# A mixture-of-experts router's product, turned round and laid between the transposes of a layer norm

## The chip, the cores and the metric

One NeuronCore of a Trainium2 chip runs the whole program in one launch. The metric is the device time of one execution in microseconds (us). The core's engines run side by side, each in the order of its own instructions, and wait for one another by semaphores: TensorE (PE; its weight loads are listed apart as PEld), VectorE (DVE), ScalarE (ACT), GpSimdE (POOL), and SyncE (SP), which issues most of the loads.

## The reference, cut to what matters

512 tokens with 1024 features pass through two layers of one kind of block and then two of another. The change is in the second kind, between its first layer norm and its experts:

```python
def route(x2, w_router, router_bias):                 # x2: 512 x 1024
    scores = jax.nn.sigmoid(jnp.einsum('nd,de->ne', x2, w_router))   # 512 x 16
    biased = scores + router_bias
    ...                                                # best group, two experts, weights
for l in range(DEPTH):                                 # DEPTH = 2
    mix = token_mixing(...)
    x = layer_norm_2(DN_ALPHA_2 * x + mix, ln1_g[l], ln1_b[l])
    ffn = moe(x.reshape(B * S, D), w_router, router_bias, w1[l], w3[l], w2[l])
    x = layer_norm_2(DN_ALPHA_2 * x + ffn, ln2_g[l], ln2_b[l])
```

Everything is float32. Which experts a token goes to is decided from these scores, so no expert's work can start before them.

## The kernel before, in words

The 512 tokens are four tiles of 128 (`NT`), the 1024 features eight blocks of 128 (`KC`). A full-precision product is made of three: each operand is split into a high part in the type fp32r and a low part (the rest), and high times high, high times low and low times high are added up in a bank of PSUM.

The layer norm is written out over three engines. VectorE (`norm_v`) handles tile after tile: it adds the rows of the residual (line 614), takes the moments (618, 622), and applies mean, gain, deviation and bias (644, 651); line 651 raises `norm_z`. TensorE (`norm_pe`, line 681) then turns the tile's eight 128x128 blocks into banks 2i and 2i+1 and raises `norm_tr` once for each bank. ScalarE (`norm_a`, line 666) copies a bank into `xT_hi`, the high part with features on the partitions and tokens on the free axis, and VectorE (line 627) makes `xT_lo` and raises `norm_lo`. ScalarE takes its deviations two tiles ahead (line 661), in order, so it makes the high part of tile i only when tile i+2 has its variance. On VectorE the low part of tile i-1 stands behind line 651 of tile i and the variance of tile i+1.

After the norm comes the router, on TensorE at lines 2024 to 2034: wait for all eight low parts; 24 products (lines 468 to 470, `triple`) with the router's weights (128x16) stationary and 512 tokens moving, into 16 rows of bank 0; wait for the sigmoid that ScalarE writes into `scT` (line 2272, 16x512); turn `scT` back in four transposes of 16x128 (line 2033) into bank 2. VectorE copies that to `rsc` (line 2494, 128x64) and starts a chain of small operations: the bias (2497), the best group, two best experts as one-hot rows (up to 2540). TensorE ranks the tokens with two products (2037, 2038), VectorE works out the slots, TensorE places them (2042), and GpSimdE gathers the rows of the experts' tokens. The experts' first products (2070) follow.

Ahead of the router, ScalarE issues four loads on its own queue: the next norm's gain and bias, then `rbias` (2269) and `row128` (2270). VectorE waits for the last two before line 2497. The router's weights are loaded and split by GpSimdE in the ring of weight units; that is done before the norm ends.

Of the kernel before, what the change touches and what calls it, by code (L numbers as in the profile page):

```python
# [20 lines left out]
P = 128  # L21
S = 512
NT = S // P
D = 1024
KC = D // P
# [6 lines left out]
ACT = mybir.ActivationFunctionType  # L32
# [18 lines left out]
NE, NG = 16, 4  # L51
NOV = 2 * S // P
NB = NOV + NE
RAW, SPLIT = 4, 2
# [9 lines left out]
def shape_constants():  # L64
# [75 lines left out]
    "m_t": (0, 0, 16),  # L140
    "m_o": (0, 0, 16),
    "a_ot": (0, 0, 4),
    "rt_tr": (0, 0, 1),
    "rt_rank": (0, 0, 1),
    "slot_mm": (0, 0, 1),
    "gb_ld": (2, 4, 4),
# [37 lines left out]
    "h_hi": (0, 0, 17),  # L184
    "y_ev": (0, 0, 33),
    "gt_use": (0, 0, 26),
    "v_step": (24, 237, 343),
    "norm_var": (4, 8, 8),
    "norm_z": (4, 8, 8),
    "norm_lo": (8, 16, 16),  # L190
# [211 lines left out]
class Feed:  # L402
# [3 lines left out]
    RAW, SPLIT = 12, 4  # L406
# [59 lines left out]
def triple(pe, out, wh, wl, xh, xl, first, last):  # L466

    pe.matmul(out, wh, xh, start=first, stop=False)
    pe.matmul(out, wh, xl, start=False, stop=False)
    return pe.matmul(out, wl, xh, start=False, stop=last)  # L470


def flat(ap):
    return ap.rearrange("p a b -> p (a b)")
# [6 lines left out]
def build(nc, t, out):  # L481

    ctx = ExitStack()
    with ctx:
# [6 lines left out]
        def signal(name, step=1):  # L491
            return Signal(name, sem(name), step)
# [3 lines left out]
        h = sb("h", [P, NT, D])  # L496
        xT_hi = sb("xT_hi", [P, KC, S], F32R)
        xT_lo = sb("xT_lo", [P, KC, S], F32R)
        ring = Stream(sb, sem)
# [15 lines left out]
        eps, unit1 = small[:, 0:1], small[:, 1:2]  # L515
        ident = konst[:, K_ID:K_ID + P]
        bank = [ctx.enter_context(nc.psum_tensor(f"bank{i}", [P, S], F32)) for i in range(8)]
# [49 lines left out]
        v_step, a_step = signal("v_step"), signal("a_step")  # L567
# [3 lines left out]
        norm_var, norm_sd, norm_z = signal("norm_var"), signal("norm_sd"), signal("norm_z")  # L571
        tile_sum = signal("tile_sum")
        norm_tr, norm_hi, norm_lo = signal("norm_tr"), signal("norm_hi"), signal("norm_lo")
# [84 lines left out]
        def norm_a(A, n):  # L658
# [12 lines left out]
            for i in range(NT):  # L671
                if i + 2 < NT:
                    deviation(i + 2)
                high(i)

        def norm_pe(T, n):
            for i in range(NT):
                T.eng.wait_ge(norm_z.sem, norm_z.at(T, NT * n + i + 1))
                for x in range(2):
                    for k in range(4):  # L680
                        last = T.eng.transpose(bank[2 * i + x][:, k * P:k * P + P],  # L681
                                               h[:, i, (4 * x + k) * P:(4 * x + k + 1) * P], ident)
                    last.then_inc(norm_tr.sem, norm_tr.up(T))

        def load_gb(A, g_row, b_row):
            A.eng.dma_start(gb[:, 0, :], over(g_row, [P, D])).then_inc(gb_ld.sem, gb_ld.up(A))
# [616 lines left out]
        def vector1(V):  # L1303
# [240 lines left out]
        U2_IW, U2_V, U2_MK, U2_PW, U2_MV, U2_G, U2_OUT, U2_R = 5, 14, 26, 30, 31, 35, 83, 91  # L1544
# [37 lines left out]
        s7 = lambda name, shape, dt=F32: sb(name, shape, dt, moe)  # L1582
# [11 lines left out]
                      for w, x in ((wt_hi, xT_hi), (wt_lo, xT_lo))))  # L1594
        yg = [wt[:, i, :] for i in range(2 * NT)]
        rsc, rbi = s7("rsc", [P, NT, NE]), s7("rbi", [P, NT, NE])
        scT, row128 = s7("scT", [NE, S]), s7("row128", [P, P])
        rgs, ghot, rbest = s7("rgs", [P, NT, NG]), s7("ghot", [P, NT, NG]), s7("rbest", [P, NT, 1])
        slot_ge, slot_b, slot_p = (s7(n, [P, 2 * NT, w]) for n, w in (("slot_ge", NB + 2), ("slot_b", NB + 1), ("slot_p", P)))
        hot2, d128 = s7("hot2", [P, NT, NE]), s7("d128", [P, 2 * NT])  # L1600
# [3 lines left out]
        gw = s7("gw", [P, NT, 4])  # L1604
# [31 lines left out]

        m_s, m_mx, m_p, m_t, m_te, m_o = (signal(n) for n in ("m_s", "m_mx", "m_p", "m_t", "m_te", "m_o"))

        gt_sig, gt_use, mg_hi, mg_lo, rt_sc, rt_oh, rt_rank, rt_dest, be_ok, rt_tr, slot_oh, slot_mm = (signal(n) for n in (
            "gt_sig", "gt_use", "mg_hi", "mg_lo", "rt_sc", "rt_oh", "rt_rank", "rt_dest", "be_ok", "rt_tr", "slot_oh", "slot_mm"))  # L1640

        x_tr, x_hi, x_lo, act_h, h_val, h_tr, h_hi, h_lo, y_ev, yg_use = (signal(n) for n in (
            "x_tr", "x_hi", "x_lo", "act_h", "h_val", "h_tr", "h_hi", "h_lo", "y_ev", "yg_use"))
# [164 lines left out]
        def tensor2(T):  # L1808
            pe = T.eng
# [38 lines left out]
            for c in range(ROPED):  # L1848
# [5 lines left out]
                if c == 4:  # L1854
                    wh, wl = (w[:, 0:64].rearrange("p (k c) -> p k c", k=KC) for w in ring.weights(T, U2_IW))
# [16 lines left out]
            for j in range(4):  # L1872
                wh, wl = ring.weights(T, U2_V + j)
# [147 lines left out]
            for _ in dense:  # L2021
                pass
            rows_products(T, U2_OUT, KC, xT_hi, xT_lo, mg_lo)
            norm_pe(T, 0)
            T.eng.wait_ge(norm_lo.sem, norm_lo.at(T, 8))

            wh, wl = (w[:, 0:P].rearrange("p (k e) -> p k e", k=KC) for w in ring.weights(T, U2_R))
            for k in range(KC):
                last = triple(pe, bank[0][0:NE, :], wh[:, k, :], wl[:, k, :], xT_hi[:, k, :], xT_lo[:, k, :], k == 0, k == 7)
            last.then_inc(ring.done, 1)  # L2030
            T.eng.wait_ge(rt_sc.sem, T.alone(rt_sc.at(T, 1)))
            for i in range(NT):
                last = pe.transpose(bank[2][:, NE * i:NE * i + NE], scT[:, i * P:i * P + P], ident[0:NE, 0:NE])
            last.then_inc(rt_tr.sem, rt_tr.up(T))
            T.eng.wait_ge(rt_oh.sem, rt_oh.at(T, 1))

            pe.matmul(bank[1][:, 0:NT * NE], konst[:, K_TRF:K_TRF + P], flat(oh[:, 2, :, :]), start=True, stop=True)
# [113 lines left out]
        def scalar2(A):  # L2151
# [116 lines left out]
            load_gb(A, t["ln2_g_2"][bass.ds(l, 1), :], t["ln2_b_2"][bass.ds(l, 1), :])  # L2268
            act.dma_start(rbias[:], over(t["router_bias_2"].rearrange("(o n) -> o n", o=1), [P, NE])).then_inc(rb_ld.sem, rb_ld.up(A))
            act.dma_start(row128[:], t["konst"][:, K_END:K_END + P]).then_inc(rb_ld.sem, rb_ld.up(A))  # L2270
            A.eng.wait_ge(ring.done, ring.products(A, U2_R))
            act.activation(scT[:], bank[0][0:NE, :], ACT.Sigmoid).then_inc(rt_sc.sem, rt_sc.up(A))

            def x_high(e):
                for y in range(2):
# [48 lines left out]
        def vector2(V):  # L2324
            v = V.eng
# [164 lines left out]
                v.tensor_tensor(xT_lo[:, k, :], merged[k], xT_hi[:, k, :].bitcast(F32), SUB).then_inc(mg_lo.sem, mg_lo.up(V))  # L2490
            norm_v(V, 0, U2_OUT + KC - 1)

            V.eng.wait_ge(rt_tr.sem, rt_tr.at(V, 1))
            v.tensor_copy(flat(rsc[:]), bank[2][:, 0:NT * NE]).then_inc(v_step.sem, v_step.up(V))
            V.eng.wait_ge(v_step.sem, v_step.last(V))
            V.eng.wait_ge(rb_ld.sem, rb_ld.at(V, 2))
            v.tensor_tensor(rbi[:], rsc[:], over(rbias[:].unsqueeze(1), [P, NT, NE]), ADD).then_inc(v_step.sem, v_step.up(V))
            V.eng.wait_ge(v_step.sem, v_step.last(V))
# [327 lines left out]
```

## Time and profile before

| | |
|---|---|
| time, median of 3 runs | 3400.06 us (3392.2 to 3403.74) |
| the profiled execution | 3393.37 us, its span 3391.6 us |
| mean granted clock of TensorE | 0.928 of full |
| PE / PEld busy | 2981.4 us (88%) / 2356.0 us (69%) |
| DVE / ACT / POOL busy | 1815.1 / 1381.4 / 1145.3 us |
| the chain that ended last, by engine | PE 57%, issue 20%, DVE 9%, POOL 8%, ACT 3% |

The span runs from the first to the last instruction of the profiled execution. The granted clock is the share of TensorE's full clock (2.4 GHz) that the chip lets through; it is 1.00 or 0.50 at any moment, so the engine works at 2.4 or at 1.2 GHz. Busy times count an engine's instructions, for PE with ends that overlap. The chain is followed back from the last instruction, at each step to what released it. Times of a row are counted from the start of the span.

### The profile page before, as it was taken

Reading aid. Unit: us, or ns where it says so; the run is one execution under the profiler, and the core shown is the slowest. Engines: PE = TensorE matmul, PEld = TensorE weight load, DVE = VectorE, ACT = ScalarE, POOL = GpSimd, SP = SyncE. Lnnn points to the kernel's source line nnn. Section 1 sums busy time; section 2 is a strip of 40 time slices with the busy share of each in tenths; the row PEclk is TensorE's granted clock in tenths of the full one; section 3 lists DMA queues with packets and bytes.
Section 4 is the critical chain, followed back from the end, with each engine's and each line's share of the span. In section 5 each row is a group of like instructions: output and inputs, shape, how many; then the busy total and the mean of one; then the engine's idle time right before and its main releaser. Section 6 shows DMA issues by size and latency. Waiting matters only on the chain.

```text
span 3391.6 us, 44938 instructions
## 1 busy us (share of the span) xinstructions
PE 2981.4 (88%) x13284; PEld 2356.0 (69%) x13284; DVE 1815.1 (54%) x2681; ACT 1381.4 (41%) x1973; POOL 1145.3 (34%) x699
## 2 busy tenths in 40 slices
PE   6887899979987999889999976999499999959994
PEld 4666688866756888766777764887357777738883
DVE  3774434035754432246544246998556533159996
ACT  3523455215342553111244214887121343118883
POOL 2213344533123445433743530110345543611101
PEclk8998899989988999988999987999699999969996
DMA  3211233522112334322322335998222322339993
GB/s 111 64 34 62 81 99 93 173 68 70 38 53 76 94 99 137 119 69 57 103 66 57 85 142 199 411 411 334 91 67 72 94 57 68 99 141 383 411 411 146
DMA packets 373732, 461.46 MB, mean 136 GB/s; under 512 B 33396, under 2 KB 280262, under 8 KB 373512
## 3 DMA queue, kind: packets, MB, share of 16 engines
q1 hardware_dynamic: 353664, 392.05, 34.3%
q0 software_dynamic: 14976, 54.53, 4.2%
q10 hardware_dynamic: 4872, 12.26, 1.0%
q8 instruction: 100, 1.64, 0.2%
q14 instruction: 120, 0.98, 0.1%
HBM read 423.10 MB, written 35.65 MB: 135 GB/s over the span
## 4 chain that ended last, share of the span: by engine, by line
PE 57%; issue 20%; DVE 9%; POOL 8%; ACT 3%; DMA 1%; POOLq 0%; DVEq 0%; ACTq 0%; SPq 0%
PE bank L462 8%; PE bank L463 7%; POOL unit_lo L382 6%; PE bank L1935 4%; PE bank L2070 3%; PE bank L2071 3%; PE bank L2074 3%; PE bank L701 2%; PE bank L2084 2%; PE bank L2088 2%; PE bank L2085 2%; DVE u L1343 2%; PE bank L797 2%; PE bank L798 1%; PE bank L800 1%
## 5 line engine op out<-in xcount | busy, mean ns | idle before, releaser
L462 PE MATMUL bank<-xT_hi,unit_hi 128*128 128x512 f32 x1680 | 692.1, 412 | 20.7 <-DVE xT_lo L627 10.5
L463 PE MATMUL bank<-xT_lo,unit_hi 128*128 128x512 f32 x1680 | 664.9, 396 | 0.0
L382 POOL TENSOR_TENSOR unit_lo<-unit_raw,unit_hi 128x1024 fp32r<-128x1024 f32 (+1 forms) x168 | 402.6, 2396 | 762.9 <-ACT unit_hi L375 762.9
L365 POOL TENSOR_SCALAR unit_hi<-unit_raw 128x1024 fp32r<-128x1024 f32 (+1 forms) x208 | 201.7, 970 | 759.5 <-PE bank L1935 303.3
L367 POOL TENSOR_TENSOR unit_lo<-unit_raw,unit_hi 128x1024 fp32r<-128x1024 f32 (+1 forms) x208 | 442.2, 2126 | 17.4
L462 PEld LDWEIGHTS bank<-xT_hi,unit_hi 128*128 128x128 f32 x1680 | 322.2, 192 | 119.7 <-issue 42.7
L463 PEld LDWEIGHTS bank<-xT_lo,unit_hi 128*128 128x128 f32 x1680 | 322.3, 192 | 70.6 <-issue 7.3
L375 ACT ACTIVATE unit_hi<-unit_raw 128x1024 fp32r<-128x1024 f32 (+1 forms) x168 | 176.7, 1052 | 415.9 <-PE bank L701 174.6
L701 PE MATMUL bank<-xT_hi,unit_lo 128*128 128x512 f32 x1040 | 256.9, 389 | 0.0
L447 DVE TENSOR_TENSOR wt_lo<-wt,wt_hi 128x1024 fp32r<-128x1024 f32 x192 | 229.2, 1222 | 33.0 <-ACT wt_hi L442 32.1
L681 PE MATMUL bank<-konst,h 128*128 128x128 f32 x288 | 69.0, 419 | 201.6 <-DVE h L651 201.6
L447 DVE TENSOR_TENSOR xT_lo<-wt,xT_hi 128x1024 fp32r<-128x1024 f32 x192 | 234.5, 1223 | 12.5 <-ACT xT_hi L442 2.7
L442 ACT ACTIVATE xT_hi<-wt 128x1024 fp32r<-128x1024 f32 x192 | 203.6, 1063 | 50.8 <-PE bank L2074 32.5
L701 PEld LDWEIGHTS bank<-xT_hi,unit_lo 128*128 128x128 f32 x1040 | 195.2, 188 | 40.5
L614 DVE SCALAR_TENSOR_TENSOR h<-h,bank 128x512 f32<-128x512 f32 x48 | 30.6, 678 | 353.1 <-PE bank L800 353.1
L442 ACT ACTIVATE wt_hi<-wt 128x1024 fp32r<-128x1024 f32 x192 | 200.4, 1063 | 33.0 <-PE bank L2074 27.5
L681 PEld LDWEIGHTS bank<-konst,h 128*128 128x128 f32 x288 | 55.0, 218 | 216.2 <-DVE h L651 209.2
L1524 DVE SCALAR_TENSOR_TENSOR cv<-bank,pcol,cv 128x511 f32<-128x511 f32 x88 | 66.0, 750 | 242.5 <-ACT cv L1258 242.5
L1753 POOL DMA_INDIRECT xb<-h_rows,slots x32 | 44.0, 1376 | 383.3 <-PE bank L2049 243.1
L661 ACT ACTIVATE sd<-mv,small 128x1 f32<-128x1 f32 x36 | 10.6, 295 | 364.8 <-DVE mv L622 364.8
L797 PE MATMUL bank<-unit_hi,g_hi 128*128 128x512 f32 x352 | 137.4, 390 | 3.6 <-POOL unit_lo L382 3.6
L798 PE MATMUL bank<-unit_hi,g_lo 128*128 128x512 f32 x352 | 137.0, 389 | 0.0
(453 smaller groups left out, 6204.6 us busy)
## 6 DMA issues: line engine op xcount, KB each, us to landing
wt<-in_w SPq DMA_DIRECT2D x384, 512.0 KB, 8.1
unit_raw<-in_w_in SPq DMA_DIRECT2D x276, 256.0 KB, 3.1
unit_raw<-in_w_ffn_up SPq DMA_DIRECT2D x176, 256.0 KB, 3.1
unit_raw<-in_w_ffn_down SPq DMA_DIRECT2D x88, 256.0 KB, 3.1
unit_raw<-in_w_out SPq DMA_DIRECT2D x64, 256.0 KB, 2.8
y_rows<-yb POOLq DMA_DIRECT2D x32, 512.0 KB, 7.3
y_rows<-zeros POOLq DMA_DIRECT2D x24, 512.0 KB, 5.2
unit_raw<-in_w_br SPq DMA_DIRECT2D x96, 128.0 KB, 2.2
```

What stands on the lines that cost most here:

```text
L365: pool.eng.tensor_scalar(hi, raw, 1.0, 0.0, MUL, ADD).then_inc(self.hi_made, 1)
L367: pool.eng.tensor_tensor(lo, raw, hi.bitcast(F32), SUB).then_inc(self.split, 1)
L375: act.eng.activation(self.hi[j % SPLIT][:, 0:width], self.raw[j % RAW][:, 0:width], ACT.Copy).then_inc(self.hi_made, 1)
L382: pool.eng.tensor_tensor(lo, raw, hi.bitcast(F32), SUB).then_inc(self.split, 1)
L442: act.eng.activation(self.hi[n % self.SPLIT], self.raw[n % self.RAW], ACT.Copy).then_inc(self.hi_made, 1)
L447: dve.eng.tensor_tensor(self.lo[n % self.SPLIT], self.raw[n % self.RAW], self.hi[n % self.SPLIT].bitcast(F32), SUB).then_inc(self.split, 1)
L462: pe.matmul(out, wh, xh, start=first, stop=False)
L463: pe.matmul(out, wh, xl, start=False, stop=False)
L701: last = T.eng.matmul(out_bank[:, 0:n], wl[:, k, :], xh[k], start=False, stop=k == kc - 1)
L797: T.eng.matmul(o, x_hi[:, row, c], wh[:, n], start=k == 0, stop=False)
L798: T.eng.matmul(o, x_lo[:, row, c], wh[:, n], start=False, stop=False)
L1935: last = pe.matmul(o, wl[:, k, :], ah[k], start=False, stop=k == kc - 1)
```

## The change: what it does

The roles of the operands are exchanged. A tile of 128 tokens (of `xT_hi` or `xT_lo`) is stationary and the router's 16 columns move, so that the scores come out with tokens on the partitions, 16 columns of bank 0 for each tile. The product of tile i-1 stands in TensorE's order between the transposes of tile i and those of tile i+1; the last two products follow the last transposes. ScalarE takes one sigmoid of 128x64 straight into `rsc`, and VectorE waits for that. `scT`, the four transposes back, their semaphore and VectorE's copy are gone. ScalarE takes a sigmoid of one column into an unused column of `gw` ahead of its wait for the product.

```diff
+        def turned_rows(T, n, i):
+            T.eng.wait_ge(norm_z.sem, norm_z.at(T, NT * n + i + 1))
+            for x in range(2):
+                for k in range(4):
+                    last = T.eng.transpose(bank[2 * i + x][:, k * P:k * P + P],
+                                           h[:, i, (4 * x + k) * P:(4 * x + k + 1) * P], ident)
+                last.then_inc(norm_tr.sem, norm_tr.up(T))
+
         def norm_pe(T, n):
             for i in range(NT):
-                ...
+                turned_rows(T, n, i)
...
-            norm_pe(T, 0)
-            T.eng.wait_ge(norm_lo.sem, norm_lo.at(T, 8))
-
-            wh, wl = (w[:, 0:P].rearrange("p (k e) -> p k e", k=KC) for w in ring.weights(T, U2_R))
-            for k in range(KC):
-                last = triple(pe, bank[0][0:NE, :], wh[:, k, :], wl[:, k, :], xT_hi[:, k, :], xT_lo[:, k, :], k == 0, k == 7)
-            last.then_inc(ring.done, 1)
-            T.eng.wait_ge(rt_sc.sem, T.alone(rt_sc.at(T, 1)))
+            def routed(i):
+                c = slice(i * P, i * P + P)
+                T.eng.wait_ge(norm_lo.sem, norm_lo.at(T, 2 * i + 2))
+                if i == 0:
+                    T.eng.wait_ge(ring.split, ring.split_is(T, U2_R))
+                wh, wl = (w[U2_R % SPLIT][:, 0:P].rearrange("p (k e) -> p k e", k=KC) for w in (ring.hi, ring.lo))
+                o = bank[0][:, i * NE:i * NE + NE]
+                for k in range(KC):
+                    pe.matmul(o, xT_hi[:, k, c], wh[:, k, :], start=k == 0, stop=False)
+                    pe.matmul(o, xT_hi[:, k, c], wl[:, k, :], start=False, stop=False)
+                    last = pe.matmul(o, xT_lo[:, k, c], wh[:, k, :], start=False, stop=k == KC - 1)
+                if i == NT - 1:
+                    last.then_inc(ring.done, 1)
+
             for i in range(NT):
-                last = pe.transpose(bank[2][:, NE * i:NE * i + NE], scT[:, i * P:i * P + P], ident[0:NE, 0:NE])
-            last.then_inc(rt_tr.sem, rt_tr.up(T))
+                turned_rows(T, 0, i)
+                if i:
+                    routed(i - 1)
+            routed(NT - 1)
...
+            act.activation(gw[:, 0, 3:4], unit1, ACT.Sigmoid)
             A.eng.wait_ge(ring.done, ring.products(A, U2_R))
-            act.activation(scT[:], bank[0][0:NE, :], ACT.Sigmoid).then_inc(rt_sc.sem, rt_sc.up(A))
+            act.activation(flat(rsc[:]), bank[0][:, 0:NT * NE], ACT.Sigmoid).then_inc(rt_sc.sem, rt_sc.up(A))
...
-            V.eng.wait_ge(rt_tr.sem, rt_tr.at(V, 1))
-            v.tensor_copy(flat(rsc[:]), bank[2][:, 0:NT * NE]).then_inc(v_step.sem, v_step.up(V))
-            V.eng.wait_ge(v_step.sem, v_step.last(V))
+            V.eng.wait_ge(rt_sc.sem, rt_sc.at(V, 1))
```

## Rows read from the trace of the kernel before

**Rows 1.** The page: shares of the chain that ended last, by engine.
```profile
PE 57%; issue 20%; DVE 9%; POOL 8%; ACT 3%; DMA 1%; POOLq 0%; DVEq 0%; ACTq 0%; SPq 0%
```
**Rows 2.** The chain, first layer's router: start us, us, engine, tile, line.
```profile
2031.89 1.30 DVE h L651
2033.23 1.98 PE bank L681 x8
...
2035.87 0.70 DVE xT_lo L627
2036.69 0.60 PE bank L468
...
2043.48 0.25 PE bank L470
2043.75 0.60 ACT scT L2272
2044.48 0.40 PE bank L2033 x4
2044.90 0.24 DVE rsc L2494
2045.16 0.24 DVE rbi L2497
```
**Rows 3.** The chain, second layer's router.
```profile
3004.79 1.30 DVE h L651
...
3018.01 0.23 DVE rbi L2497
```
**Rows 4.** The timeline of the first layer's norm: start, us, engine, line, operation.
```profile
2021.32 1.97 PE L681 MATMUL bank<-konst,h 128*128 128x128 f32 x8 [4.36 <-DVE h L651]
2022.23 1.29 DVE L627 TENSOR_TENSOR xT_lo<-bank,xT_hi 128x512 fp32r<-128x512 f32 x2 [0.84 <-ACT xT_hi L666]
...
2028.41 1.97 PE L681 MATMUL bank<-konst,h 128*128 128x128 f32 x8 [5.12 <-DVE h L651]
2029.32 1.29 DVE L627 TENSOR_TENSOR xT_lo<-bank,xT_hi 128x512 fp32r<-128x512 f32 x2 [0.85 <-ACT xT_hi L666]
2033.10 1.28 DVE L627 TENSOR_TENSOR xT_lo<-bank,xT_hi 128x512 fp32r<-128x512 f32 x2
```
**Rows 5.** The timeline of TensorE where the slots are placed.
```profile
2060.68 3.61 PE L2042 MATMUL bank<-slot_b,slot_p 128*128 128x25 f32 x16 [7.64 <-DVE slot_p L2593]
```
**Rows 6.** The timeline of TensorE in an earlier stage with 256 columns moving.
```profile
1650.61 1.12 PE L701 MATMUL bank<-b_hi,unit_lo 128*128 128x256 f32 x8
```
**Rows 7.** Groups by form: busy us, mean ns of one, idle before.
```profile
L2042 PE MATMUL bank<-slot_b,slot_p 128*128 128x25 f32 x32 | 7.2, 390 | 15.3 <-DVE slot_p L2593 15.3
...
L701 PE MATMUL bank<-b_hi,unit_lo 128*128 128x256 f32 x64 | 9.4, 289 | 0.7 <-POOL unit_lo L367 0.5
...
L469 PEld LDWEIGHTS bank<-c_lo,unit_hi 128*128 128x128 f32 x8 | 1.5, 189 | 0.7 <-issue 0.5
...
L469 PEld LDWEIGHTS bank<-xT_lo,unit_hi 128*8 128x8 f32 x16 | 1.4, 88 | 2.2
```
**Rows 8.** Windows: stretch, its us, busy (count) of PE, PEld, DVE, ACT, POOL; PEclk, DMA share, GB/s.
```profile
2022.40:2029.40 7.00, 1.88 (x10) 1.48 (x9) 6.15 (x11) 1.18 (x4) 0.00 (x0) 0.50 0.17 70
2036.60:2039.40 2.80, 2.71 (x7) 0.99 (x8) 0.00 (x0) 1.28 (x1) 0.00 (x0) 0.50 0.95 334
2039.60:2043.70 4.10, 4.10 (x18) 1.52 (x16) 0.00 (x0) 0.00 (x0) 0.00 (x0) 1.00 0.10 26
2060.60:2064.30 3.70, 3.61 (x16) 3.49 (x16) 0.02 (x1) 0.00 (x0) 0.00 (x0) 0.50 0.00 0
```
**Rows 9.** ScalarE and its queue ahead of the sigmoid, by the timeline.
```profile
2036.64 0.45 ACTq L2270 DMA_DIRECT2D row<-in_konst  x1
...
2037.19 1.28 ACT L2272 ACT_TABLE_LOAD   x1 [1.35 <-issue]
```
**Rows 10.** The tile `row128`: issue to landing in both layers.
```profile
DMA to landing us min/median/max: 4.1/4.9/5.8
```

More of the change, by code:

```diff
@@ L142 @@
     "a_ot": (0, 0, 4),
-    "rt_tr": (0, 0, 1),
     "rt_rank": (0, 0, 1),
@@ L186 @@
     "gt_use": (0, 0, 26),
-    "v_step": (24, 237, 343),
+    "v_step": (24, 237, 342),
     "norm_var": (4, 8, 8),
@@ L674, in norm_a @@
                 high(i)
+        def turned_rows(T, n, i):
[5 more added lines that the diff above has]
+                last.then_inc(norm_tr.sem, norm_tr.up(T))
         def norm_pe(T, n):
             for i in range(NT):
[L678 to L683, printed above, removed]
+                turned_rows(T, n, i)
         def load_gb(A, g_row, b_row):
@@ L1596, in build @@
         rsc, rbi = s7("rsc", [P, NT, NE]), s7("rbi", [P, NT, NE])
-        scT, row128 = s7("scT", [NE, S]), s7("row128", [P, P])
+        row128 = s7("row128", [P, P])
         rgs, ghot, rbest = s7("rgs", [P, NT, NG]), s7("ghot", [P, NT, NG]), s7("rbest", [P, NT, 1])
@@ L1637, in build @@
         m_s, m_mx, m_p, m_t, m_te, m_o = (signal(n) for n in ("m_s", "m_mx", "m_p", "m_t", "m_te", "m_o"))
-        gt_sig, gt_use, mg_hi, mg_lo, rt_sc, rt_oh, rt_rank, rt_dest, be_ok, rt_tr, slot_oh, slot_mm = (signal(n) for n in (
-            "gt_sig", "gt_use", "mg_hi", "mg_lo", "rt_sc", "rt_oh", "rt_rank", "rt_dest", "be_ok", "rt_tr", "slot_oh", "slot_mm"))
+        gt_sig, gt_use, mg_hi, mg_lo, rt_sc, rt_oh, rt_rank, rt_dest, be_ok, slot_oh, slot_mm = (signal(n) for n in (
+            "gt_sig", "gt_use", "mg_hi", "mg_lo", "rt_sc", "rt_oh", "rt_rank", "rt_dest", "be_ok", "slot_oh", "slot_mm"))
         x_tr, x_hi, x_lo, act_h, h_val, h_tr, h_hi, h_lo, y_ev, yg_use = (signal(n) for n in (
```

## The prediction
> **What bounds the kernel now.** I read the page first, then the chain of waits around the router, then the timeline of the norm ahead of it, then windows for TensorE's clock. The page's chain gives PE 57% of the span, VectorE 9% and ScalarE 3% [rows 1], so a change in one stage has to be read in that stage. At the router the chain passes through every instruction that the change touches: line 651 of the last tile, eight transposes, the last high and low part, 24 products from 2036.69 to 2043.73, the sigmoid, four transposes back, VectorE's copy, and the bias at 2045.16 [rows 2]. Nothing runs beside it that the end waits for, and the ranks, the slots, the gather and the experts follow from it. So what is gained or lost at line 2497 shows whole in the span, once in each of the two layers. The distance from line 651 of the last tile to line 2497 is 13.27 us in the first layer [rows 2] and 13.22 us in the second [rows 3]: one calculation serves both.
>
> The norm ahead of it is VectorE's. The transposes of tiles 1, 2 and 3 start at 2021.32, 2028.41 and 2033.23, each for some 2 us, and TensorE stands idle in between [rows 2, 4]. The low parts of tiles 0, 1, 2 and 3 are done at 23.52, 30.61, 34.38 and 36.57 (times of two digits are 2000 us and more) [rows 2, 4]. TensorE's clock is at 0.50, that is 1.2 GHz, all through these gaps [rows 8].
>
> **What goes.** From the end of the last product to line 2497 there are now 45.16 - 43.73 = 1.43 us: the sigmoid of 16x512 0.60, the transposes 0.40, the copy 0.24, and hand-overs [rows 2]. After the change one sigmoid of 128x64 stands there. Its 64 elements a partition are an eighth of 512. The trace has no such form; it costs between 0.1 and 0.6, and I take 0.3, as VectorE's 64-element operations cost 0.24 [rows 2]; with hand-overs 0.4. So 1.0 us goes (bounds 0.75 to 1.25). The table load of 1.28 us at 2037.19 was already hidden ahead of the wait [rows 9], and the one-column sigmoid follows it there: nothing gained, nothing lost, unless the product ended before 38.8.
>
> **What the product costs.** 24 instructions become 96, in four groups of 24, each with a weight load of 128 columns and 16 columns moving. Before, 512 moving columns covered a load of 16; now there is next to nothing to cover a load of 128. What does such a pair cost? The trace has no fp32r product with so few columns. Nearest is line 2042, 128 columns loaded and 25 moving, in f32: 16 of them in 3.61 us, the last with its own 0.39, so (3.61 - 0.39) / 15 = 0.215 us from start to start, at the low clock [rows 5, 7, 8]. Is fp32r as slow? At the full clock its load takes 189 ns for 128 columns and 88 ns for 8 [rows 7]: 0.84 ns a column, two cycles of 2.4 GHz. For 128 columns that is 108 ns at the full clock and 215 ns at the low one, the same as line 2042. From below the bound is four transposes with a load of 128 columns of 16 rows in 0.40 us, about half of it the last one's own time, so some 0.06 each at the full clock, 0.12 at the low one [rows 2, 8]. From above it is eight products with 256 moving columns in 1.12 us at the full clock, the last with its own 0.29, so 0.12 each, or 0.24 at the low one [rows 6, 7]. I take 0.215, being closest to line 2042, so 5.2 us for a tile at the low clock, 20.6 for the four, where 7.04 stood before.
>
> The Trainium skill, TensorE: Matmul & The Clock Gate, section "LDWEIGHTS (loading the stationary operand)", gives a load as its columns divided by 1.2 nanoseconds, so 107 ns for 128, and does not double it for this type or at the low clock. By it the four groups would take 10 us. Line 2042 at the low clock is twice that, so I put the row first, and the page's number is a rival below.
>
> **Which clock?** The product before raised it: from 2036.60 to 2039.40 PE is busy 2.71 of 2.80 us at 0.50, and after that the rows show 1.00 [rows 8]. But line 2042 keeps PE busy for 3.61 of 3.70 us with few columns moving, and the clock stays at 0.50 [rows 8]. The new product looks like line 2042, not like the old one. I take 0.50 throughout.
>
> **Where it lies.** TensorE works in order, so each group also stands in front of the next transposes.
> - Tile 0's product may start when its low part is made: 23.52 plus the 0.12 seen between the low part and the first product, 23.65. It ends at 28.8. Tile 2's transposes are due at 28.41, so they start 0.4 late, and TensorE is free at about 30.55. Their high parts are used by VectorE only at 33.10: hidden.
> - Tile 1's product waits for 30.61, starts at 30.7 and ends at 35.9. Tile 3's transposes were ready at 33.23. They now wait behind it: 2.7 us late. This is the new stall. Behind them on ScalarE stand the last high parts and the four loads of its queue, on VectorE the last low part: 36.57 becomes 39.3.
> - Tile 3's transposes hold TensorE for 1.7 us, to 37.6. Tile 2's product follows to 42.8, tile 3's to 48.0; nothing more is waited for, since the low part of 39.3 is long there. The last result comes 0.39 after its start, at 48.1.
> - Sigmoid and hand-overs 0.4: line 2497 at 48.5 against 45.16, which is 3.3 us later.
>
> In words: from 30.7 on TensorE has three groups of 5.2 us and one set of transposes in a row, 17.3 us, where it had the transposes and 7.04 us of products, most of them at the full clock. Nearly all of the overlap with the norm is eaten by 13.6 us more work (20.6 - 7.04). The loads of ScalarE's queue are issued 2.7 us later; `row128` took 5.8 us at most from its issue at 36.64 [rows 9, 10], so it is there at 45.1, ahead of 48.5. Its own moved DMAs, and the row stores that SP issues on `norm_z`, are hidden. The ring's semaphore for the router's unit is raised later, and no one else is due on it. The clock is at 0.50 for the ranks and slots in both cases [rows 8], so nothing follows there.
>
> **The sum.** 2 x 3.3 = 6.6 us on the profiled 3393.4: 3400.0. That execution is 6.7 under the median of 3400.06, so for a median I say 3406.7, in round figures 3406.
>
> **The rivals.**
> - *The clock rises.* If the dense new product lifts the clock as the old one did, a group costs 24 x 0.11 = 2.6 us from the second or third on. Tile 1's product ends at 33.4, the transposes of tile 3 start 0.2 late and go twice as fast, tile 2's product runs from 34.4 to 37.0, tile 3's to 39.6, line 2497 could go at 40.1. But then VectorE waits for `row128`: issued at 36.6, landed at 42.4 in the first layer and at the equal of 40.8 in the second [rows 9, 10]. Gain 2.7 + 4.3 = 7.0 us; time 3393. For it: the old product did so at the same share of busy time. Against it: line 2042. This is the case on the other side, and it turns on whether the granted clock reaches 1.00 before tile 2's product. The same page of the Trainium skill, section "What's actually happening", says that the throttled clock is the default and that activity releases it, which speaks for this rival if a busy PE with few columns counts as activity.
> - *Loads are cheaper than I think.* At 0.12 a pair, at the low clock, a group is 2.9 us: tile 0's ends at 26.6, tile 1's at 33.6, the last two run from 35.4 to 41.2, line 2497 is at 41.7, held in the first layer by `row128` to 42.4. Gain 2.7 + 3.5 = 6.2; time 3394. For it only the four small transposes, which load 16 rows. It decides below some 0.17 us a pair: 30.7 + 24 x 0.17 = 34.8, 1.5 late, the end at 44.7, as before.
> - *Something else than the product decides*, such as a landing or a phase of the experts' loads, and takes or gives a few us. Nothing in the chain points to one.
>
> **How the numbers follow.** Forecast 0.68, clock rises 0.15, cheaper loads 0.12, something else 0.05. A measurement of this kernel can tell some 0.3%, that is 10.2 us, from no change; all three cases lie within it. A quarter of the forecast's sizes (pairs up to 0.24: 24 x 0.025 x 3 = 1.8 us a layer more) and the spread of the runs (11.5 us from lowest to highest before) carry 0.14 of it beyond 10.2 us slower, and about a quarter of the two rivals beyond 10.2 faster. So faster 0.08, same 0.77, slower 0.15. The range takes in both rivals' 3393, less 4 for spread, and the top of the forecast, 3406 + 4 + 4: 3389 to 3414. The forecast's own range is 3401 to 3413.
>
> **What would show it.** In the changed profile: 96 products a layer, 0.215 us from start to start; windows over them at 0.50; tile 3's transposes some 2.7 us after line 651 instead of 0.06; from line 651 of the last tile to line 2497 16.6 us instead of 13.3; no wait of VectorE for `row128`. A granted clock of 1.00 over the last two groups, or pairs at 0.12, would make it wrong, and then line 2497 should stand 8 to 11 us behind line 651.

## The result, and the profile after

Over 20 runs each the changed kernel takes 3403.47 us in the median (3399.06 to 3408.27), the kernel before 3399.14 us (3392.20 to 3404.79). The ratio is 1.0015 with a 95% interval from 1.0008 to 1.0022: 5.1 us slower, between 2.7 and 7.5. That is real, and within the 0.3% that the forecast called no change. The profiled execution took 3403.39 us, its span is 3401.6 us.

The page's chain by engine has hardly moved (before: [rows 1]):

```profile
PE 58%; issue 20%; DVE 9%; POOL 8%; ACT 3%; DMA 1%; POOLq 0%; ACTq 0%; DVEq 0%; SPq 0%
```

The timeline of the first layer's norm and router in the changed kernel (start us, us, engine, line, operation, idle before and what ended it). Line numbers have shifted: 681 is now 679, 651 is 650, 627 is 626, 2497 is 2507; the product is lines 2035 to 2037.

```profile
2023.45 0.38 PE L2035 MATMUL bank<-unit_hi,xT_hi 128*128 128x16 f32 x1 [0.36 <-DVE xT_lo L626]
...
2028.38 0.36 PE L2037 MATMUL bank<-unit_hi,xT_lo 128*128 128x16 f32 x1
...
2028.59 1.97 PE L679 MATMUL bank<-konst,h 128*128 128x128 f32 x8
...
2030.47 0.38 PE L2035 MATMUL bank<-unit_hi,xT_hi 128*128 128x16 f32 x1
...
2031.70 1.28 DVE L650 SCALAR_TENSOR_TENSOR h<-h,rs,gb 128x1024 f32<-128x1024 f32 x1
...
2035.40 0.36 PE L2037 MATMUL bank<-unit_hi,xT_lo 128*128 128x16 f32 x1
...
2035.61 1.97 PE L679 MATMUL bank<-konst,h 128*128 128x128 f32 x8
...
2037.23 0.36 PE L2035 MATMUL bank<-unit_hi,xT_hi 128*128 128x16 f32 x1
...
2038.24 0.69 DVE L626 TENSOR_TENSOR xT_lo<-bank,xT_hi 128x512 fp32r<-128x512 f32 x1 [0.16 <-ACT xT_hi L665]
...
2039.50 1.28 ACT L2282 ACT_TABLE_LOAD   x1 [1.29 <-issue]
...
2040.80 0.20 ACT L2282 ACTIVATE gw<-small 128x1 f32<-128x1 f32 x1
...
2047.26 0.36 PE L2037 MATMUL bank<-unit_hi,xT_lo 128*128 128x16 f32 x1
2047.65 0.23 ACT L2284 ACTIVATE rsc<-bank 128x64 f32<-128x64 f32 x1 [6.66 <-PE bank L2037]
...
2047.91 0.22 DVE L2507 TENSOR_TENSOR rbi<-rsc,rbias 128x64 f32<-128x64 f32 x1 [8.98 <-ACT rsc L2284]
```

Read it beside [rows 2, 4]. Tile 0's product begins at 2023.45, as soon as its low part is made, and its last instruction starts at 2028.38. Tile 2's transposes follow at 2028.59. Tile 1's product begins at 2030.47, and its last instruction starts at 2035.40, while line 650 of tile 3 began at 2031.70 and was done at 2032.98: the transposes of tile 3 start only at 2035.61, without a gap behind the product, where they stood 0.06 us behind line 651 before. Then come two more groups of 24 in a row, and the last result meets a sigmoid of 0.23 us and, 0.26 after its start, the bias add at 2047.91. From line 650 (651 before) of the last tile to that add it is 16.21 us instead of 13.27 [rows 2]. The second layer repeats it: 3027.94 - 3011.74 = 16.20, instead of 13.22 [rows 3].

```profile
3011.74 1.28 DVE L650 SCALAR_TENSOR_TENSOR h<-h,rs,gb 128x1024 f32<-128x1024 f32 x1
...
3027.94 0.22 DVE L2507 TENSOR_TENSOR rbi<-rsc,rbias 128x64 f32<-128x64 f32 x1 [8.98 <-ACT rsc L2284]
```

Windows over tile 0's, tile 1's and the last two products (columns as in [rows 8]): PE and PEld are both busy without a hole, and the granted clock is 0.50 in all three.

```profile
2023.40:2028.60 5.20, 5.14 (x25) 5.15 (x25) 4.88 (x7) 0.29 (x2) 0.00 (x0) 0.50 0.00 0
2030.40:2035.60 5.20, 5.20 (x25) 5.13 (x24) 3.75 (x6) 0.60 (x1) 0.00 (x0) 0.50 0.27 107
2037.20:2047.40 10.20, 10.20 (x50) 10.20 (x48) 1.38 (x2) 2.24 (x4) 0.00 (x0) 0.50 0.34 110
```

Groups by form in the changed kernel. The weight load takes 333 ns, nearly the 361 ns of the product itself. Both are longer than the 0.213 us from one start to the next, since neighbouring instructions overlap in the trace.

```profile
L2036 PE MATMUL bank<-unit_lo,xT_hi 128*128 128x16 f32 x64 | 23.1, 361 | 0.0
...
L2036 PEld LDWEIGHTS bank<-unit_lo,xT_hi 128*128 128x128 f32 x64 | 21.3, 333 | 0.0
```

### The profile page after: what moved, and what is told of

Its sections match the earlier page's. It is cut to its first block, busy times and chain, and to the rows that moved or that the text cites. A ratio compares the mean times of both kernels' runs of the same rounds, so it can differ in the third digit from the quotient of the medians.

```text
span 3401.6 us, 45212 instructions
## 1 busy us (share of the span) xinstructions
PE 3008.8 (88%) x13420; PEld 2392.2 (70%) x13420; DVE 1814.6 (53%) x2679; ACT 1381.3 (41%) x1975; POOL 1144.1 (34%) x699
## 4 chain that ended last, share of the span: by engine, by line
PE 58%; issue 20%; DVE 9%; POOL 8%; ACT 3%; DMA 1%; POOLq 0%; ACTq 0%; DVEq 0%; SPq 0%
PE bank L461 8%; PE bank L462 7%; POOL unit_lo L381 6%; PE bank L1937 4%; PE bank L2081 3%; PE bank L2082 3%; PE bank L2085 3%; PE bank L703 2%; PE bank L2095 2%; PE bank L2099 2%; PE bank L2096 2%; DVE u L1345 2%; PE bank L799 2%; PE bank L800 1%; PE bank L802 1%
## 5 line engine op out<-in xcount | busy, mean ns | idle before, releaser
L660 ACT ACTIVATE sd<-mv,small 128x1 f32<-128x1 f32 x36 | 10.6, 295 | 363.9 <-DVE mv L621 363.9
```

## The experiments

The kernel before ran beside each of them on the same chip, with medians of 3398.6 to 3400.9, and the ratios are to those runs. "Distance" is always from the start of line 651 (or its like) of the last tile to the start of the bias add in the first / second layer, in us.

| kernel | median | ratio to before (95%) | distance |
|---|---|---|---|
| before | 3399.14 | 1 | 13.27 / 13.22 |
| changed | 3403.47 | 1.0015 (1.0008 to 1.0022) | 16.21 / 16.20 |
| products behind all transposes | 3417.46 | 1.0051 (1.0037 to 1.0066) | 23.88 / 23.88 |
| transposes of tile 3 first | 3404.14 | 1.0015 (1.0005 to 1.0025) | 16.21 / 16.21 |
| weights stationary, same places | 3392.08 | 0.9980 (0.9970 to 0.9990) | 9.17 / 8.99 |
| 128 columns moving | 3397.14 | 0.9989 (0.9980 to 0.9998) | 16.31 / 12.34 |
| weights stationary, early row128 | 3388.70 | 0.9966 (0.9951 to 0.9980) | 8.09 / 8.07 |
| the same, TensorE kept busy | 3381.63 | 0.9947 (0.9934 to 0.9961) | 7.06 / 7.06 |
| the same, busy behind the product only | 3379.86 | 0.9937 (0.9922 to 0.9952) | 8.03 / 8.06 |
| 128 columns, kept busy in the norm | 3394.43 | 0.9981 (0.9971 to 0.9991) | 11.44 / 11.49 |
| 16 columns, kept busy in the norm | 3401.05 | 1.0009 (0.9998 to 1.0021) | 14.53 / 14.53 |
| before, with pure delay | 3403.46 | 1.0007 (0.9998 to 1.0016) | 16.28 / 17.51 |

**The four products behind all transposes.**

```diff
-            for i in range(NT):
-                turned_rows(T, 0, i)
-                if i:
-                    routed(i - 1)
-            routed(NT - 1)
+            norm_pe(T, 0)
+            for i in range(NT):
+                routed(i)
```

> The changed kernel with its four products moved behind all transposes. Theory (a pair of load and product costs 0.213 us at the low clock, the clock stays at 0.50, and TensorE's work is what the end waits for): 96 x 0.213 = 20.5 us in one piece behind the last low part, so line 651 of the last tile to the bias add is 3.4 + 0.1 + 20.5 + 0.7 = 24.7 us instead of 16.0 in the changed kernel: 8.7 us a layer more, some 17 us slower than the changed kernel, 0.6 to 0.7% slower than the kernel before. Rival (a dense row of products lifts the clock once it is long enough): the granted clock reaches 1.00 inside the 20 us, the rest runs at 0.11, and the distance is 14 to 17 us.

```profile
2034.90:2055.30 20.40, 20.29 (x97) 20.20 (x95) 1.21 (x2) 2.16 (x4) 0.00 (x0) 0.50 0.17 60
```

One piece of 20.3 us, the 96 products and the end of a transpose, at the low clock from end to end (in the second layer 20.34 us busy in a stretch of 20.40, again at 0.50), and a distance of 23.88, 7.7 us more than in the changed kernel. The forecast was 24.7, and the clock did not rise in 20 us of dense narrow products. So the interleaving of the change gives back 7.7 us a layer; it pays for part of a product that has become 13.4 us longer.

**The transposes of tile 3 inside tile 1's product.**

```diff
+            turned_rows(T, 0, 2)
+            routed(1, (0, KC // 2))
+            turned_rows(T, 0, 3)
+            routed(1, (KC // 2, KC))
+            routed(2)
+            routed(3)
```

> The changed kernel with the transposes of tile 3 laid into the middle of tile 1's product, after its fourth block of eight. Theory (work of TensorE, not the order): the transposes start at once behind line 651, the last low part is made some 2.3 us earlier, and the bias add comes at the same time, within 0.2 us a layer of the changed kernel, since TensorE has the same instructions in a row without a gap. Rival (the stall of 2.4 us in front of tile 3's transposes is the loss): the bias add comes 2.3 us earlier in each layer, and the time is 4 to 5 us under the changed kernel's.

```profile
2033.04 1.97 PE L679 MATMUL bank<-konst,h 128*128 128x128 f32 x8
...
2035.67 0.69 DVE L626 TENSOR_TENSOR xT_lo<-bank,xT_hi 128x512 fp32r<-128x512 f32 x1 [0.16 <-ACT xT_hi L665]
...
2047.90 0.23 DVE L2512 TENSOR_TENSOR rbi<-rsc,rbias 128x64 f32<-128x64 f32 x1 [11.54 <-ACT rsc L2289]
```

The transposes now start at 2033.04 instead of 2035.61 and the last low part at 2035.67 instead of 2038.24, both 2.57 us sooner, and the bias add stands at 2047.90 instead of 2047.91. The stall in front of tile 3's transposes is real and costs nothing by itself: from 2030.5 on TensorE has 72 pairs and eight transposes to do in any order. The rival falls.

**The weights stationary again, in the places of the change.**

```diff
-                o = bank[0][:, i * NE:i * NE + NE]
+                o = bank[0][0:NE, c]
                 for k in range(KC):
-                    pe.matmul(o, xT_hi[:, k, c], wh[:, k, :], start=k == 0, stop=False)
-                    ...
+                    last = triple(pe, o, wh[:, k, :], wl[:, k, :], xT_hi[:, k, c], xT_lo[:, k, c], k == 0, k == KC - 1)
...
+            T.eng.wait_ge(rt_sc.sem, T.alone(rt_sc.at(T, 1)))
+            ...                                        # four transposes back, sigmoid into scT, copy to rsc
```

> Places of the changed kernel, operands of the kernel before: the router's 16 columns stationary, 128 tokens of one tile moving, sigmoid of 16x512, four transposes back and VectorE's copy, with the sigmoid's table loaded early. Theory (the load of 128 columns is the cost): a load of 16 hides under 128 moving columns, 24 x 0.107 = 2.6 us a tile at the low clock; the last product ends at 40.3 on the scale of the first layer, the bias add could go at 41.8, and waits for row128 to 42.4 in the first layer: 2.7 + 3.4 us earlier than the kernel before, 11 to 12 us under the changed kernel, so 0.15 to 0.2% faster than the kernel before. Rival (narrow products cost 0.21 us whatever is stationary): no faster than the changed kernel, and 1 us a layer slower for the way back.

```profile
2031.88 0.29 PE L468 MATMUL bank<-xT_hi,unit_hi 128*16 128x128 f32 x1 [0.99 <-DVE xT_lo L627]
...
2034.31 0.31 PE L470 MATMUL bank<-xT_hi,unit_lo 128*16 128x128 f32 x1
...
2034.45 1.97 PE L680 MATMUL bank<-konst,h 128*128 128x128 f32 x8
...
2037.87 0.45 ACTq L2284 DMA_DIRECT2D row<-in_konst  x1
...
2042.29 0.23 DVE L2512 TENSOR_TENSOR rbi<-rsc,rbias 128x64 f32<-128x64 f32 x1 [1.16 <-DMA row<-in_konst]
```

Tile 1's product runs from 2031.88 to 2034.31, 24 starts of 0.107 us at the low clock, and the transposes of tile 3 are due just then. The clock then rises at 2037.2 and the rest goes at 0.059 a start:

```profile
2031.80:2034.50 2.70, 2.62 (x25) 2.52 (x25) 2.67 (x5) 0.16 (x1) 0.00 (x0) 0.50 0.04 12
2037.20:2040.00 2.80, 2.50 (x41) 2.32 (x39) 0.58 (x1) 1.63 (x3) 0.00 (x0) 0.99 0.84 317
```

The last line of the timeline shows VectorE waiting 1.16 us for the landing of `row128`, which the forecast had named as the next thing late in its fast cases. The expectation came to distances of 10.6 and 9.8; measured are 9.17 and 8.99. In the first layer the bound was `row128`, taken to land 5.8 us after its issue, and it took 4.3. In the second it was the end of the product, which came sooner by the risen clock. So the places of the change were worth having and the exchange of operands was not: with the same places and the old operands the distance falls by 4.1 us and 4.2 us against before, with the new ones it rises by 2.9.

**128 columns moving: eight copies of the 16.**

```diff
+                eight = lambda w: over(w.unsqueeze(1), [P, 8, NE])
-                    pe.matmul(o, xT_hi[:, k, c], wh[:, k, :], start=k == 0, stop=False)
+                    pe.matmul(o, xT_hi[:, k, c], eight(wh[:, k, :]), start=k == 0, stop=False)
```

> The changed kernel with 128 columns moving instead of 16: eight copies of the router's 16, of which one is used. Theory (load-bound): 0.213 us from start to start as with 16 columns, at the low clock; the time is the changed kernel's within 0.1%, unless the wider products lift the clock, in which case the pairs fall to 0.11 and the bias add comes up to 5 us earlier a layer. Rival (a fixed cost and the columns behind one another): 0.213 + 112 / 1.2 GHz = 0.307 us a pair, 2.2 us a tile more, some 7 us a layer slower.

```profile
2042.30 0.41 PE L2037 MATMUL bank<-unit_lo,xT_hi 128*128 128x128 f32 x1
2042.51 0.41 PE L2038 MATMUL bank<-unit_hi,xT_lo 128*128 128x128 f32 x1
```

From start to start it is 0.21 us with eight times the columns (0.213 with 16), so the moving columns are not what a pair waits for. Nor is it a fixed cost of an instruction: with 16 columns loaded and 128 moving it was 0.107 at the same clock. What is left is the load of 128 columns, with the moving ones under it. In the first layer the distance is 16.31, as with 16 columns. In the second the clock rose 2 us into the last two products, which the narrow ones never saw without fill, and the distance fell to 12.34:

```profile
2037.50:2048.00 10.50, 10.50 (x50) 10.36 (x49) 1.38 (x2) 2.28 (x4) 0.00 (x0) 0.50 0.30 107
3013.70:3020.40 6.70, 6.62 (x51) 6.48 (x49) 1.38 (x2) 2.36 (x5) 0.00 (x0) 0.84 0.50 168
```

The profiled distances don't explain this kernel's time. Their sum is 2.2 us more than in the kernel before, and yet the median is lower, 0.9989 (0.9980 to 0.9998), 0.7 to 6.8 us faster. Whether the clock rises in both layers in most executions, or another stage gives the rest, one profile can't tell.

**rbias and row128 ahead of the norm**, on top of the kernel with stationary weights.

```diff
+            A.eng.wait_ge(mg_lo.sem, mg_lo.at(A, KC))
+            act.dma_start(rbias[:], ...)
+            act.dma_start(row128[:], ...)
             norm_a(A, 0)
```

> The kernel with the weights stationary, laid between the transposes (9.1 us from line 651 to the bias add), and with rbias and row128 issued by ScalarE ahead of the norm instead of behind it. Theory (the landing of row128 was the last wait of VectorE there, by 1.16 and 0.9 us): the distance falls to 8.0 us in both layers, some 2 us in all, 0.05%; the time is about 3390. Rival (another wait stands right behind it): less than half of that.

```profile
2039.96 0.59 ACT scT L2288
...
2040.69 0.41 PE bank L2047 x4
2041.12 0.23 DVE rsc L2510
2041.38 0.23 DVE rbi L2513
```

The chain now goes through sigmoid, transposes back and copy to the bias add, with no wait for a load: 8.09 / 8.07, 1.1 and 0.9 us less, as expected. The time went from 0.9980 to 0.9966 of before, with intervals that overlap: the gain is shown by the distances and not by the time.

**TensorE kept busy.** Products of 512 columns whose result no one reads fill its gaps.

```diff
+            def warm(b, n):
+                w = ring.hi[(U2_R - 1) % SPLIT]
+                for _ in range(n):
+                    pe.matmul(bank[b][:], w[:, 0:P], w[:, 0:S], start=True, stop=True)
...
+                if i == 2:
+                    warm(1, 3)
                 if i:
                     routed(i - 1)
+                    if i < 3:
+                        warm(1, (8, 3)[i - 1])
...
+            warm(7, 22)                                # ahead of the wait for the one-hot rows
+            warm(7, 28)                                # ahead of the wait for the slots
+            warm(7, 44)                                # behind the slots
```

> The same, with products of 512 columns that no one reads filled into TensorE's gaps in the norm (8, 3 and 3 in a layer) and in the routing behind it (22, 28 and 44), so that the granted clock stays at 1.00. Theory (the low clock is a price of its own in this stage): from line 651 to the bias add 7.0 us instead of 8.0, the two ranking products 0.4 us, the eight slot products 1.7 us and the first expert's products some 2 us shorter: 4 to 5 us a layer, 8 to 10 in all, so about 3381. Rival (the fill stands in front of what the chain waits for, or the clock falls all the same): no gain or a loss; each group of fill that meets the low clock costs twice its time, 3 to 9 us.

```profile
2035.70:2042.30 6.60, 6.22 (x81) 5.47 (x82) 5.02 (x7) 2.71 (x5) 0.00 (x0) 1.00 0.46 152
2044.00:2051.00 7.00, 5.13 (x24) 3.94 (x22) 5.66 (x31) 3.00 (x4) 0.00 (x0) 1.00 0.04 13
2051.00:2059.00 8.00, 8.00 (x31) 6.53 (x31) 6.67 (x28) 0.00 (x0) 0.00 (x0) 0.79 0.00 0
2059.00:2062.00 3.00, 3.00 (x23) 2.78 (x22) 0.75 (x3) 0.00 (x0) 0.00 (x0) 1.00 0.00 0
```

The clock is 1.00 over tile 1's to tile 3's products and again where the slots are placed; between, it is 0.79 over 8 us. The distance falls to 7.06 in both layers, and the time to 0.9947, 3381.63 us, as expected. By the profiles the stage behind the bias add is only 2.6 and 1.3 us shorter than without fill, so with the distance a layer gives 3.6 and 2.3 us instead of 4 to 5.

> The weights-still kernel with early row128, with the fill in the routing behind the product alone (22, 28, 44) and none in the norm. Theory (the two fills work apart from each other: the first makes the product short, the second keeps the clock for ranks, slots and the first experts): the distance from line 651 to the bias add stays at 8.1 us, and the rest of the gain of the kernel kept busy in both places, 3 to 4 us a layer, is kept, so some 3383 us. Rival (the second fill starts at the low clock and stands in front of the ranks): 22 products of 0.43 us are 9.4 us against a gap of 6.8, up to 2.6 us later a layer, no gain over the kernel without fill.

With the fill behind the product alone the distance goes back to 8.03 / 8.06 and the time, 0.9937, is no worse (3379.86 against 3381.63, from two sets of runs with overlapping intervals). The fill in the norm is worth 1 us of distance a layer and is not seen in the time. This is the fastest version that ran: 0.63% under the kernel before, some 21 us, and 8.8 us under the kernel without fill by the medians.

Where this gain lies is only in part what the expectation said, 3 to 4 us a layer behind the router. In the profiles of the two, the stage from the bias add to the first sum of experts' rows takes 337.0 us with the fill and 340.7 without it in the first layer, but 336.5 and 336.6 in the second. The other 3.3 us between the two spans lie in the untouched stage of the next section. The chain shows the price in the second layer, with the fill of 44 (line 2030) in it:

```profile
3024.58 11.44 PE bank L2030 x44
3036.02 0.46 PE bank L2075 x4
```

In the kernel without fill the chain goes through the landing of the rows there:

```profile
3034.68 5.55 DMA xb<-h_rows,slots
...
3040.28 1.99 PE bank L2063 x8
```

The slots are placed 1.8 us sooner behind the bias add, but the fill then holds TensorE up to 28.8 us behind it, where without fill the rows had landed at 26.1. The first product of the experts starts at 31.3 instead of 29.6. In the first layer, where the rows landed only at 30.1 without fill, it starts at 31.3 instead of 33.6. So 44 is too many for the second layer, and a shorter fill was not tried.

**The same fill in the norm, with tokens stationary**, 128 and then 16 columns moving; both with `row128` early, and with 8 and 3 fill products.

> The changed orientation with 128 columns moving (eight copies), row128 issued early, and the same fill in the norm's gaps alone (8 and 3). Theory (wide products hold the clock, a load of 128 columns is 0.107 us at 1.00): a group takes 2.6 us, from line 651 to the bias add 8 to 9 us in both layers instead of 16.3 and 12.3. Rival (the clock depends on the moment at which the stretch begins, and the fill doesn't change that): one layer or both stay above 12 us.

> The changed kernel itself (16 columns moving), with row128 issued early and the same fill of 8 and 3. Theory (a dense row of narrow products does not hold the clock up): the fill lifts the clock, tile 0's product lets it fall again, and the last two groups run at 0.213 us a pair; the distance stays at 14 to 16.5 us. Rival (any dense work holds it once it is up): 8 to 9 us, as with wide products.

Windows of the kernel with 128 columns: the fill of eight, tile 1's product, the last two.

```profile
2030.80:2034.30 3.50, 3.50 (x10) 2.66 (x10) 2.96 (x5) 0.96 (x2) 0.00 (x0) 0.50 0.37 150
2036.00:2038.60 2.60, 2.60 (x25) 2.57 (x23) 1.02 (x2) 0.20 (x1) 0.00 (x0) 1.00 0.50 202
2039.40:2045.00 5.60, 5.60 (x51) 5.49 (x49) 1.29 (x2) 2.49 (x4) 0.00 (x0) 1.00 0.55 187
```

Windows of the kernel with 16: the fill of eight, tile 1's product, the beginning of tile 2's, tile 3's.

```profile
2028.30:2032.00 3.70, 3.70 (x11) 2.82 (x11) 3.03 (x5) 1.09 (x3) 0.00 (x0) 0.50 0.35 142
2033.60:2036.20 2.60, 2.60 (x25) 2.56 (x24) 1.05 (x2) 0.22 (x1) 0.00 (x0) 1.00 0.50 202
2037.10:2039.00 1.90, 1.90 (x20) 1.90 (x19) 1.29 (x2) 1.62 (x3) 0.00 (x0) 1.00 0.24 91
2040.40:2045.60 5.20, 5.20 (x26) 5.20 (x25) 0.00 (x0) 0.00 (x0) 0.00 (x0) 0.50 0.20 68
```

Wide or narrow, 24 pairs take 2.6 us at 1.00, half of their 5.1 at 0.50. The wide ones hold the clock to the end. Under the narrow ones it falls at 2039.0, in the middle of tile 2's group, and tile 3's group is back at 5.2 us. So the rival of a rising clock had its price right, 2.6 us a group; the narrow products neither raised the clock without fill nor kept it once the fill had raised it. The narrow kernel's distance of 14.53 lies in the range expected. The wide one's missed it, 11.4 instead of 8 to 9, since the fill of eight met the low clock, held TensorE for 3.5 us and made tile 2's transposes and all behind them late: the cost of fill at the wrong moment.

**Pure delay in the kernel before**: six more sigmoids ahead of the one that counts.

```diff
+            for b in (1, 3, 4, 5, 6, 7):
+                act.activation(bank[b][0:NE, :], bank[0][0:NE, :], ACT.Sigmoid)
             act.activation(scT[:], bank[0][0:NE, :], ACT.Sigmoid).then_inc(rt_sc.sem, rt_sc.up(A))
```

> The kernel before with nothing changed but six more sigmoids of 16x512 (into banks of PSUM that no one reads then) ahead of the one that counts, some 6 x 0.5 = 3.0 us of pure delay on the chain in each layer. Theory (what the change costs is the 2.96 us a layer by which the bias add is late, handed on whole): the distance from line 651 to the bias add is 16.2 us and the time is the changed kernel's, 0.1 to 0.2% over the kernel before. Rival (the experts' stage takes a late start back, and the changed kernel is slower for another reason): within 0.05% of the kernel before.

The distances came out 3.0 us and 4.3 us longer, and the time at 1.0007 (0.9998 to 1.0016). The six sigmoids take 2.9 us in each layer. The second layer's other 1.3 us are the product's, which was not touched: there 13 of its 24 instructions went at the low clock before it rose, instead of 6.

```profile
2037.90:2044.90 7.00, 6.86 (x24) 2.52 (x24) 0.01 (x1) 1.28 (x1) 0.00 (x0) 0.79 0.45 154
3017.80:3026.00 8.20, 8.03 (x24) 2.86 (x24) 0.04 (x1) 1.28 (x1) 0.00 (x0) 0.63 0.37 130
```

Handed on whole, the profiled delay would be 7.3 us, 1.0021, and the sigmoids alone 5.8 us, 1.0017. Both lie above the interval, which reaches 1.0016, the second only just. The interval also overlaps the changed kernel's, and no effect at all. So this run doesn't bear out that such a delay is handed on whole, and neither shows how much of it is given back, nor where.

## Why the prediction was right

**The cost of a pair.** The step that carried the forecast put 0.215 us at the low clock from line 2042 [rows 5, 7], two cycles a column for the load. Measured 0.213 from start to start, with a load of 333 ns as on line 2042 itself. The experiments with 128 columns moving, once with 128 and once with 16 loaded, show together that it is the load. The figure of the page of the Trainium skill that the forecast named (TensorE: Matmul & The Clock Gate, "LDWEIGHTS (loading the stationary operand)", 107 ns for 128 columns) meets what the chip does at the full clock for this type (24 pairs in 2.6 us) and is half of what it does at the low one.

**The clock.** It was put at 0.50 throughout, since line 2042 kept PE busy and did not raise it [rows 8]. So it was, in both layers, and even in 20 us in a row. The rival needed 1.00 before tile 2's product; this never came without fill. The old product has 512 moving columns to a load, and raised it; the eight copies have 128, and raised it in one layer of two. The same page of the Trainium skill, "What's actually happening", holds here in that fill raised the clock (the two kernels with fill in the norm and tokens stationary); the 20.29 us of narrow products in 20.40 us did not.

The reason that the forecast gave was thinner than its outcome. It rested on 3.7 us of line 2042 at 0.50. But the old product, too, went at 0.50 for 2.9 us in the kernel before and for 5.9 us in the second layer of the kernel with pure delay, and then the clock rose. A row of 3.7 us could not exclude that, so in the forecast the choice was in part luck; the 20 us in a row are what settled it.

**Where it lies.** Forecast against measured, on the first layer's scale (the changed trace runs 0.19 us ahead there, which is left in): tile 1's product 30.7 to 35.9, 30.47 to 35.6; tile 3's transposes 2.7 late, 35.61 against 33.23, so 2.4 (2.6 with the offset); last low part done at 39.3, 38.9; last result 48.1, 47.6; bias add 48.5, 47.91. The distance was forecast as 16.6 and is 16.21: some 0.2 from the pairs (5.14 and 5.12 us a group where 5.2 was taken), 0.1 from the transposes (1.62 us instead of 1.7), the rest from the start and the tail, where the sigmoid took 0.23 instead of 0.3. The loss a layer, 3.3 forecast, is 2.9 and 3.0. The table load ended at 2040.78 and the one-column sigmoid at 2041.0, hidden as said. From the bias add to the end of the slots it is 19.13 us in both kernels, so there, too, nothing followed.

**The sum.** 6.6 us was said, the distances add up to 2.94 + 2.98 = 5.9, and the medians differ by 4.3, the ratio by 5.1 (2.7 to 7.5). Direction and size were right, the size a little high. Several of the other kernels follow the sum of their two distances, with 3399 us for the ratios: 21.3 us more gave 17.3 more (12.6 to 22.4), 8.3 less gave 6.8 less (3.4 to 10.2), 10.3 less gave 11.6 less (6.8 to 16.7). Two do not: the eight copies, 2.2 us more and 3.7 us less in time (6.8 to 0.7), and the pure delay, 7.3 us more and 2.4 us more in time (0.7 less to 5.4 more). So the step of the forecast that what is lost at the bias add shows whole in the span is borne out only roughly. One step was not in the forecast: the two profiled spans differ by 10.0 us, not by 5.9. The rest lies in an untouched stage, where the clock was low for 6.8 us before and for 20.5 us after:

```profile
2541.00:2565.00 24.00, 22.66 (x71) 13.32 (x70) 8.65 (x10) 1.56 (x3) 5.79 (x4) 0.86 0.08 22
```

```profile
2541.00:2565.00 24.00, 20.79 (x35) 10.22 (x36) 4.64 (x8) 2.39 (x4) 0.00 (x0) 0.57 0.08 22
```

The two windows cover the same 24 us of each span, at 0.86 and 0.57. The experts' stage of the first layer, from the bias add to the first sum of experts' rows (line 2663), is 1.6 us shorter, 340.4 instead of 342.0; from that sum to the last tile's line 651 in the second layer it is 617.6 us before and 623.4 after. The other profiles go with their low clock from 2440 to 2900: 10.2 us of it gives 616.7, 13.7 gives 617.6 (the kernel before), 20.5 gives 620.1 to 620.8, 23.9 gives 621.8, 27.3 gives 623.4 to 624.1, and 34.1 gives 626.6, some half a microsecond for each microsecond. Stretches like these may well be what spreads the executions of one kernel over some 10 us (before: 3392 to 3405), but each kernel was profiled once, so this is not shown; nor is it part of what the change did, as far as the medians show. Whether the shift of the stage behind the router makes the longer stretch more frequent stays open: it needs many profiles of each.

## What to carry to other kernels

A product of few columns on one side is cheap only with the few columns stationary: count the pairs and multiply by the time of a full weight load at the clock that the stretch will have, here 0.213 us at half clock, before counting what the exchange saves in transposes and copies (1.1 us here, against 13.4 us more of TensorE). Laying a product into a norm's gaps was worth it, so try place and orientation apart; and ask at once which load's landing is next, since 1 us of gain a layer was waiting for a 64 KB load that could be issued ahead of the norm. If TensorE sits at half clock in a latency chain, try products that no one reads in its gaps, and look at the chain again after: here they were worth 8.8 us by the medians, and the last 44 of them stood in the chain themselves. And read the clock of a stretch from more than one short row before a forecast rests on it.

## What was not expected of the hardware

- Narrow products kept PE busy at 0.50 for 20.3 us without raising the clock, and after it had been raised by fill they lost it again. Products with 16 columns loaded and 128 moving raised it within the same stage, and with 128 loaded and 128 moving it rose in one layer and not in the other.
- With 16 columns loaded and 128 moving in fp32r a product starts every 0.107 us at 0.50 and every 0.059 us at 1.00.
- The same 24 products of 512 columns took 7.0 us in one layer and 8.4 us in the other, in one execution, since the clock rose after 6 of them in the one and after 13 in the other (the kernel with pure delay).
- 94 products of 512 columns that no one reads, laid behind the router's product in each layer, went with a time 0.3% lower than without them (0.9937 against 0.9966, intervals that just touch), though by the profiles only 3.8 us of it lie behind the router.
